# A two-layer decoder trunk on one core: a fourth lead unit with PSUM banks of its own, a new order of the lead's work, and the opening's square sums on POOL

## What is computed

```python
x = x + 0.5 * swiglu(rms_norm(x, n_ffn1), w_gate, w_up, w_down)      # 1024 -> 2816 -> 1024
x = x + concat(gmlp_chunks(rms_norm(x, n_mix)), rg_lru(...)) @ w_out
x = x + 0.5 * swiglu(rms_norm(x, n_ffn2), ...)                       # 1024 -> 2816 -> 1024
x = x + sigmoid(rms_norm(x, n_ple) @ w_ple_gate) * (p @ w_ple_proj)
# after the last layer: rms_norm(x, n_final)
# rms_norm(x, g) = x / sqrt(mean(x*x) + eps) * g;  swiglu = (silu(x@wg) * (x@wu)) @ wd
```

## Time and profile before

| | |
|---|---|
| median of 3 runs | 1858.75 us (1858.49 to 1860.04) |
| the profiled execution | 1858.88 us |
| its span, first to last instruction | 1857.2 us |
| granted PE clock, mean | 0.994 of full |
| busy: PE, DVE, ACT, POOL | 1819.7, 1508.2, 1063.0, 299.4 us |
| PE share of the chain of waits | 89% |
| DMA: weight loads by SP | 344 of 512 KB, median 3.8 us to landing |
| DMA: accumulating loads by POOL | 104 of 512 KB, median 6.4 us to landing |
| DMA: copy_lead by POOL | 4 of 520 KB, median 3.2 us to landing |

### The profile page before, as it was taken

One profiled execution on the slowest core, in us unless ns is written; L12 is line 12 of the kernel. 1 busy time (PEld: TensorE's weight loads), 2 busy tenths in 40 slices (PEclk: granted clock), 3 DMA queues, 4 the chain that ended last, 5 costly groups with the idle time before them and its releaser, 6 DMA issues.

```text
span 1857.2 us, 37525 instructions
## 1 busy us (share of the span) xinstructions
PE 1819.7 (98%) x14824; PEld 1797.5 (97%) x14824; DVE 1508.2 (81%) x2319; ACT 1063.0 (57%) x1538; POOL 299.4 (16%) x380
## 2 busy tenths in 40 slices
PE   7999999999999999999999999999999999999997
PEld 6999999998999999999999999999999999999997
DVE  7989978768689889787689789777775897988775
ACT  6656656545456566565466565554544665655553
POOL 0011011340120110112110110115202101011122
PEclk9999999999999999999999999999999999999998
DMA  5657579722346666795355765794223657667941
GB/s 173 155 151 188 136 199 246 216 80 69 110 134 155 175 166 152 194 262 172 124 148 127 197 167 158 209 249 147 71 92 114 162 137 194 158 160 230 237 140 47
DMA packets 81265, 297.16 MB, mean 160 GB/s; under 512 B 9344, under 2 KB 11680, under 8 KB 79312
## 3 DMA queue, kind: packets, MB, share of 16 engines
q1 hardware_dynamic: 52592, 184.87, 30.9%
q0 software_dynamic: 28512, 110.03, 27.8%
HBM read 267.00 MB, written 25.74 MB: 158 GB/s over the span
## 4 chain that ended last, share of the span: by engine, by line
PE 89%; DVE 7%; issue 2%; ACT 1%; DMA 0%; DVEq 0%; SPq 0%; ACTq 0%
PE main L764 24%; PE main L730 19%; PE main L769 12%; PE aux L764 9%; PE main L926 9%; PE aux L769 5%; PE aux L926 4%; PE aux L1028 2%; PE main L819 2%; PE aux L730 1%; PE aux L976 1%; DVE w_lo L1690 1%; PE main L1028 1%; PE aux L1048 0%; DVE tmp L1854 0%
## 5 line engine op out<-in xcount | busy, mean ns | idle before, releaser
L764 PE MATMUL main<-part_hi,w_hi 128*128 128x260 f32 x1296 | 328.5, 284 | 8.8 <-DVE tmp L1854 5.3
L764 PE MATMUL main<-part_lo,w_hi 128*128 128x260 f32 x1296 | 326.6, 283 | 0.0
L764 PEld LDWEIGHTS main<-part_hi,w_hi 128*128 128x128 f32 x1296 | 244.5, 189 | 11.6 <-DVE tmp L1854 7.7
L764 PEld LDWEIGHTS main<-part_lo,w_hi 128*128 128x128 f32 x1296 | 244.5, 189 | 0.0
L622 POOL DMA_DIRECT2D w_lo<-weights_dram x104 | 90.3, 868 | 851.1 <-ACT w_lo L1154 842.5
L769 PE MATMUL main<-part_hi,w_lo 128*128 128x260 f32 x1296 | 213.7, 282 | 0.2 <-DMA w_lo<-weights_dram 0.2
L1166 ACT ACTIVATE w_hi<-tau 128x1024 fp32r<-128x1024 f32 x104 | 109.9, 1057 | 177.0 <-PE main L769 152.4
L730 PE MATMUL main<-part_hi,w_hi 128*128 128x260 f32 x944 | 192.6, 285 | 2.0 <-DVE tmp L1738 2.0
L730 PE MATMUL main<-part_hi,w_lo 128*128 128x260 f32 x944 | 189.8, 283 | 0.0
L730 PE MATMUL main<-part_lo,w_hi 128*128 128x260 f32 x944 | 189.5, 282 | 0.0
L764 PE MATMUL main<-sig,w_hi 128*128 128x260 f32 x1280 | 181.6, 284 | 5.7 <-issue 5.7
(11 more groups left out here) (325 smaller groups left out, 4544.1 us busy)
## 6 DMA issues: line engine op xcount, KB each, us to landing
raw<-weights_dram SPq DMA_DIRECT2D x344, 512.0 KB, 3.8
w_lo<-weights_dram POOLq DMA_DIRECT2D x104, 512.0 KB, 6.4
d_part<-tmp POOLq DMA_DIRECT2D x64, 260.0 KB, 5.3
x<-d_part POOLq DMA_DIRECT2D x16, 1040.0 KB, 14.3
x_spill<-x POOLq DMA_DIRECT2D x6, 1040.0 KB, 4.9
x<-x_spill POOLq DMA_DIRECT2D x6, 1040.0 KB, 9.8
x<-x_in_dram SPq DMA_DIRECT2D x4, 520.0 KB, 6.7
x<-tmp POOLq DMA_DIRECT2D x4, 520.0 KB, 3.2
```

The costliest lines, as they stand in the source:

```text
L764: pe.matmul(ps, hi_w[:, w], xx(k), start=(start and k == 0 and b == 0), stop=False, skip_group_check=True)
```

## The change

Seven things change; the arithmetic does not.

1. The fourth lead unit gets a PSUM pair of its own, `aux[1]` (the list `FOURTHS`). PE then waits for it until the square root has read `aux[1]` (`std_s`) and no longer for gate_out(0). The `main` pairs shift by one: P1(0) waits for gate_out(0), P1(1) for hidden_out(0), and no longer for hidden_out(1).
2. copy_lead becomes two DMAs of one hidden tile each, with a semaphore each.
3. On ACT copy_p1(0) goes right behind hi12(0), and h_lead(1) from in front of copy_p1(0) to behind copy_p5(0).
4. On DVE tau3, tau4, hidden_out(1) and hidden_lo(0) leave the lead of all four stages: behind lo12(0) come tau3, tau4, hidden_out(1), lo34, hidden_lo(0), lo_b; hidden_lo(1) comes behind lo12(1).
5. The sums of pair 0 (raw and high part) are made after tile 0 instead of tile 2; the low parts of pairs 0 and 1 both after tile 2.
6. In the opening POOL adds the squares 3 to 7, DVE only 1 and 2; hi(3,3) and x21(0,0) go between ACT's squares.
7. In the opening the high parts of the first pair's sums come before the square root on ACT, and their low parts before the reciprocal on DVE.

```diff
+FOURTHS = tuple(t + 1 for t in THIRDS)
...
-SUM_ORDER = ((1, 0, 2, 3), (0, 1, 2, 3))
...
-    return (g + layer + (k >= G_GT + V_AFTER) + sum(g > t for t in THIRDS)) % 2
+    return (g + layer + (k >= G_GT + V_AFTER) + sum(g > t for t in THIRDS + FOURTHS)) % 2
...
-            return aux[0] if g in THIRDS else main[main_slot(g)]
+            return aux[0] if g in THIRDS else aux[1] if g in FOURTHS else main[main_slot(g)]
...
+            def copy_lead(f, G, k):
+
+                pool.wait_ge(evac, G - 2 * (LEAD - 1 - k))
...
-                pool.dma_start(x[:, XT - 2:XT, :], tmp[:, 2:4, :]).then_inc(lead_copy, 16)
+                pool.dma_start(x[:, XT - LEAD + k, :], T(2 + k)).then_inc(lead_copy[k], 16)
...
+            for o in range(3, XT):
+                add_square(pool, 0, o)
...
                     weights_in(n + 3)
-                    pe.wait_ge(evac, G + 1)
+                    pe.wait_ge(std_s, stat + 1)
                     acc(bank(G + 3), 3, XT, x_hi, x_lo).then_inc(unit, 1)
...
                         if first and t < 2:
-                            pe.wait_ge(evac, G - 2 * (1 - t))
+                            pe.wait_ge(evac, G - 3 + t)
...
-                        if t == 1:
+                        if c and t == 1:
                             pe.wait_ge(evac, G)
...
                         if stat == 0:
-                            x21(stat, 0)
+                            sigma_hi(stat, 0)
                             root(stat)
-                            sigma_hi(stat, 0)
...
                         hi12(n, S)
+                        copy_p1(0)
                         hi34(n, S)
                         act.wait_ge(sx_lo, 2 * KH * (2 * l + which + 1))
                         hi_b(n, S)
-                        h_lead(l, G - 2 * LEAD, 1)
...
                     copy_u2(0)
                     copy_p5(0)
+                    if first:
+                        h_lead(l, G - 2 * LEAD, 1)
...
             for o in range(2, XT):
                 prep(0, o)
-            hi(3, 3)
+                if o == 4:
+                    hi(3, 3)
+                if o == 5:
+                    x21(0, 0)
...
                         elif which:
...
                             gate_out(1)
                             sigma_lo(stat, 3)
-                            ahead(1, S0, S)
-                            ahead(2, S0, S)
-                            hidden_lo(0)
-                            hidden_out(1)
+                            tau1(S0, S)
+                            tau2(S0, S)
                         else:
...
                             tau1(S0, S)
                             tau2(S0, S)
-                            hidden_out(1)
                             sigma_lo(stat, 3)
-                            tau3(S0, S)
-                            tau4(S0, S)
-                            hidden_lo(0)
...
-                        if first and t == 2:
+                        if first and t == 0:
                             sums_raw(f, c, 0)
                             sums_raw2(f, c, 0)
...
-                        if not last and t >= pairs and k % 2:
+                        if not last and t >= pairs and k % 2 and not (first and t == 1):
                             sums_lo(l, f, c, k // 2)
                         if first and t == 2:
                             sums_lo(l, f, c, 0)
+                            sums_lo(l, f, c, 1)
...
                     if first:
                         lo12(n, S)
+                        tau_sums(0, (tau3, tau4))
+                        hidden_out(1)
                         lo34(n, S)
...
+                        hidden_lo(0)
                         lo_b(n, S)
...
             add_square(dve, 0, 1)
+            add_square(dve, 0, 2)
             lo(2, 2)
-            for o in range(2, XT):
-                add_square(dve, 0, o)
             lo(3, 3)
```

More of the change, by code:

```diff
@@ L309, in trunk @@
         sh_lo = sem("sh_lo")
-        lead_copy = sem("lead_copy")
+        lead_copy = [sem(f"lead_copy{k}") for k in range(LEAD)]
         d_second = sem("d_second")
@@ L667, in gates @@
                         if c == 0 and t == 1:
-                            copy_lead(f, G)
+                            for k in range(LEAD):
+                                copy_lead(f, G, k)
                         if c and t == 1:
@@ L1603, in sums_raw @@
                 if early:
-                    dve.wait_ge(lead_copy, 16 * (f + 1))
+                    for k in range(LEAD):
+                        dve.wait_ge(lead_copy[k], 16 * (f + 1))
                 if f:
@@ L1713, in free @@
                 pending[b] = False
-            def ahead(j, n, T_):
-                if j == 1:
-                    tau1(n, T_)
-                    tau2(n, T_)
-                    tau3(n, T_)
-                if j == 2:
-                    tau4(n, T_)
-                if j == 3:
-                    lo34(n, T_)
             def ffn(l, which, u0, g0):
@@ L1926, in ffn @@
                     lo12(n + 2, S + 1)
+                    if first:
+                        hidden_lo(1)
                     c11_r(0)
```

22 lines of the change are left out of this document (9 added, 13 removed).

## The result

| | before | after |
|---|---|---|
| median | 1859.09 us (1858.49 to 1860.04, 4 runs) | 1872.26 us (1871.67 to 1873.73, 4 runs) |
| the profiled execution | 1858.88 us | 1873.73 us |
| its span | 1857.2 us | 1872.0 us |
| granted PE clock, mean | 0.994 | 0.990 |
| busy: PE, DVE, ACT, POOL | 1819.7, 1508.2, 1063.0, 299.4 us | 1825.3, 1509.2, 1062.7, 310.1 us |

The changed kernel is slower: ratio 1.0072 with a 95% interval of 1.0057 to 1.0087. The forecast of 1868.0 had the sign and the place, but the median lies 0.26 us beyond the high end of the range. The profiled execution is the slowest of the four runs shown; its span is 14.8 us longer than before's, and the medians differ by 13.2. I account for the 14.8 here and come back to the spread, since it has a cause of its own.

The account below looks back on a forecast made before the run. PE, busy nearly the whole span, was taken to bound the kernel. Terms 2.7 + 2.7 + 0.15 - 0.65 + 6.0 - 1.7 = +9.2 us on 1858.88 gave 1868; low end 1860.5, high end 1872.

Parts of the forecast that it names:

- The path: P7(0) waits for copy_u2(0), behind gate(2) on ACT, whose weight load is issued after tau4: 6.13 us from tau4's end.
- B: Layer 0's second FFN stage: P7(0) at 559.96 instead of 557.30 us, +2.7 us.
- D: Layer 1's second FFN stage: P7(0) at 1472.09 instead of 1469.43 us, +2.7 us.
- A: The opening's FFN stage: P7(0) at 52.9 instead of 53.53 us, -0.65 us.
- C: Layer 1's first FFN stage: P7(0) at 966.35 instead of 966.20 us, +0.15 us.
- the clock stays up: Rival: same PE waits, but no clock fall in B, D and A, C as now; +2.8 us, 1861.7; chance 0.16.
- Faster: Rival: copy_u2(0) does not hold P7(0), so A and C keep what the banks give; 1848 us; chance 0.12.
- POOL is late: Rival: adds of 1.87 us make PE wait 1.6 in the third lead unit, shifting A's chain; 1869.5; chance 0.08.
- clock: PE at half clock behind gaps before P7(0): 1.6 us each in A, B and D, 1.2 in C; +6.0 us.
- sums: Early sums of hidden parts shorten PE's wait on c22(4): -0.4 us in each of four stages, -1.7 in all.
- part 3, the squares: Opening's five adds moved to POOL end at 25.2 us, costing some 0.2 before the root, covered by PE's third lead unit.
- the load: Weight load for tile 2's gate cut takes 3.5 us from SP's issue to landing; bound 0.3 later per stage.

Follow-up runs that it names:

- run 1: Changed kernel with tau3 and tau4 of tile 0 back in the lead, ahead of lo12(0), in all four stages: 1857.59 us, ratio to before 0.9989.
- run 2: Kernel before with only tau3 and tau4 of tile 0 moved behind lo12(0), in all four stages: 1868.42 us, one run.
- run 3: Changed kernel with copy_u2(0) and copy_p5(0) ahead of gate(2) on ACT in the first chunk: 1857.18 us, ratio to before 0.9989.
- run 5: Changed kernel, squares still on POOL; DVE waits for them before the first pair's sums, root and reciprocal ahead of that pair's halves and low parts: 1871.86 us.
- run 4: Changed kernel with squares 3 to 7 of the opening back on DVE, in front of lo(3,3): 1870.19 us, one run.
- run 6: Changed kernel with the second copy_lead transfer later, behind POOL's load for tile 2: 1872.97 us, one run.
- run 7: Changed kernel with the sums of pair 0 back after tile 2 and the low part of pair 1 back behind tile 1: 1873.05 us.
- run 9: As run 8, but the fourth lead unit in the main pair again, with PE's waits of the kernel before: 1863.17 us, one run.
- run 8: Changed kernel with the edits of run 1, run 3 and run 4 together: 1853.93 us, ratio to before 0.9971.
- run 10: As run 8, but with tau3 and tau4 left behind lo12: 1855.88 us, ratio to before 0.9985.

## Why the prediction was right and wrong

**Right.** The path: P7(0) on copy_u2(0) behind gate(2), on a load that waits for tau4. Runs 1, 2 and 3 show it link by link. The gap at P7 in B and D with no gap before, the vanished waits on gate_out and hidden_out, P6(0) early in A and C and its gain given back at P7(0), and a lost clock behind each gap all came as described. The rival "the clock stays up" fell: the clock fell in all four stages. "Faster" did not come, for the reason given against it; run 3 shows that it was one order of ACT's program away. "POOL is late", given a chance of 0.08, came nearly whole, beside the forecast and not in its place: PE waited 1.5 us where it had 1.6, and A came 1.8 later than forecast, though with two adds of 2.16 and 2.11 us and three of 1.3 instead of five of 1.87.

Term by term, in the profiled executions (14.8 us of span against the 9.2 of the sum):

| step | predicted | measured | how it is read |
|---|---|---|---|
| A, P7(0) | -0.65 | +1.12 | 54.65 against 53.53 |
| B, P7(0) | +2.7 | +3.2 | 10.40 behind P1(0) against 7.24 |
| C, P7(0) | +0.15 | +0.45 | 12.25 against 11.11, less 0.69 by which P1(0) no longer waits for gate_out in the lead |
| D, P7(0) | +2.7 | +2.8 | 10.05 against 7.24 |
| clock | +6.0 | +8.2 | P7(0) to P1(2): A 8.62 to 10.10, B 8.67 to 10.26, C 8.98 to 11.30, D 8.67 to 11.47 |
| sums | -1.7 | -0.8 | P1(2) to P4(4): 36.08, 36.07, 36.06, 36.07 to 35.88, 35.89, 35.88, 35.85 |

The measured column adds up to 15.0, 0.2 more than the span shows; where the 0.2 goes is open.

**The step that failed: A, and in it part 3, the squares.** I had POOL's chain end at 25.2, at a cost of some 0.2, and called the third lead unit its cover. It ended at 26.26, and PE waited for it (the first row of PE's timeline above); PE's sum over partitions then ran to 27.52, and the root cannot start before that. I also had the pace of DVE unchanged, "the sum of the fourth pair 0.5 earlier (41.86)". It ended at 43.55. The first pair's sums on DVE took 5.7 us instead of 1.8. On ACT this put the first pair's halves at 26.58 and the root behind them:

```profile
26.58 0.85 ACT L1151 ACTIVATE sig<-tmp 128x780 fp32r<-128x780 f32 x1 [2.53 <-DVE tmp L1659]
27.34 0.41 ACT L1152 ACTIVATE sig<-tmp 128x260 fp32r<-128x260 f32 x1
27.65 0.68 ACT L1209 ACTIVATE rstd_b<-aux,small 128x520 f32<-128x520 f32 x1
```

In the kernel before, the root began at 26.04. So the late adds alone would have held the root until 27.5, and DVE's stretched sums held it until 27.65. Run 5 agrees: there the sums take 0.49 but wait for the adds, the root starts at 27.18, and P7(0) still at 54.70. From there the stage runs as forecast, only later: tau4 ends at 48.52 where I had 46.75, and P7(0) follows 6.13 us behind it, exactly the distance in the prediction. So the whole 1.77 us error of A lies ahead of tau4, and run 4, which takes the adds off POOL, gives 1.60 back at tau4 (0.25 of it from before the squares) and 1.30 at P7(0).

The evidence was in the trace of before. There POOL also adds squares beside DVE's sums, in its timeline in layer 0, behind the mixing stage (POOL's row first):

```profile
517.05 1.59 POOL L509 TENSOR_TENSOR sum_home<-sum_home,rs 128x520 f32<-128x520 f32 x1 [4.09 <-ACT rs L1134]
...
517.40 1.53 DVE L1642 SCALAR_TENSOR_TENSOR tmp<-x,vecs,mix 128x260 f32<-128x260 f32 x1
518.86 0.48 DVE L1644 SCALAR_TENSOR_TENSOR tmp<-x,vecs,mix 128x260 f32<-128x260 f32 x1
```

The same instruction form takes 1.53 beside an add and 0.48 behind it. I had read POOL's min, median and max of the earlier trace rows as a property of POOL's add alone, and had not asked why one instruction of one shape takes 1.30 or 1.87. The high end of the range, 1872, was to take in the later load and late adds, and both came; with the smaller gain of the sums they make 1868 + 1.8 + 1.0 + 0.9 = 1871.7, which leaves no room for the clock below.

The Trainium skill has a sentence on it (SBUF — State Buffer, section "SBUF: two separate sides"): VectorE and GpSimd share one pair of SBUF interfaces, which is an exclusive lock, so that a VectorE instruction with two SBUF inputs and a GpSimd instruction that reads SBUF wait for each other whole. The rows of this case agree, as the last section shows in numbers; the forecast had left this rule out.

**B, C and D: the load, 1.0 us in all.** I took 3.5 us from the earlier trace rows, the only load at the right place; it was 4.0, 3.8 and 3.7. The prediction had named the bound (0.3 later per stage, if it meets its neighbours) and run 6 shows some 0.3 in C and D; what slows B is open. The rest of the chain, 2.42 on DVE, held within 0.01.

**The clock, 2.2 us.** I charged a fixed 1.6 per gap, read at one gap of before. A and B came to 1.5 and 1.6; C and D to 2.3 and 2.8 in this execution, with 6.83 us at 1.2 GHz. Run 7, with gaps of the same length, had 3.41 us in both, and so had runs 4, 5 and 6. Against the 8.67 us at full clock, the stages with 3.41 us at half clock lost 1.3 to 1.6 us and those with 6.83 lost 2.6 to 2.8, and which of them comes can differ from one execution to the next (the 2.3 of C is less the 0.3 that C lost here before the change). Less these 2.2 us the profiled execution would stand at 1871.5, beside the other three at 1871.67 to 1872.72. The sum priced the cheaper case rightly, the one in B, C and D of four of the five traces with these stops; the range lacked the dear one.

**The sums, 0.9 us.** I had 0.4 a stage. The wait at c22(4) fell by 0.3 and a stop of 0.1 opened earlier, which leaves 0.2, as run 7 shows. That the gap on c22 shrinks is as forecast; its size was half.

## What to carry to other kernels

Before a pair of instructions is moved behind a wait, follow what they release: two sums of 0.68 us cost 14.7 us here, because a load was issued on their last semaphore and an unrelated copy stood behind that load's first reader. Where an in-order engine has a short copy that the bound engine needs and a long instruction that waits for a DMA, the copy goes first; that one reordering turned the changed kernel from 0.7% slower to 0.1% faster. And where a row shows one instruction of one shape with two durations, look at what the neighbour engine does in each before either is used as a price.

## What the runs showed of the hardware

**VectorE and GpSimd take turns.** An add on POOL and a DVE instruction with both inputs in SBUF wait each other out, though their rows in the trace overlap. In the opening of the changed kernel POOL's adds start at 17.51, 19.81, 22.07, 23.52 and 24.98 and end at 19.67, 21.92, 23.38, 24.83 and 26.26. DVE's instructions end at 18.50, 20.76, 22.21, 23.66, 25.12 and 26.55. Each DVE end but the first two lies 0.28 or 0.29 us behind the end of an add, and each add ends 1.14 to 1.17 behind the end of a DVE instruction. The add that starts at 17.51, during a low part of 1.22 us that ends at 18.50, takes 2.16; the low part that starts at 19.01, while that add runs, takes 1.75 and ends 1.09 behind it. The same holds at 517 us before the change: the low part ends at 517.49, the add at 518.64 (1.15 later), the sum behind it at 518.94 (0.30 later). Alone, in run 5, an add takes 1.30 and a sum 0.49. So an add costs DVE about 1.04 us of its 1.31 (1.53 less 0.49), if DVE has such work at that time. DVE instructions with one input in PSUM show none of it: in the kernel before, 26 of them (tmp<-main,rstd_b and tmp<-aux,rstd_b, 128x520) run beside an add and take 0.68 to 0.70, as elsewhere. Moving adds of 0.70 us off DVE then saves it nothing: it was spared 3.5 us (five times 0.70) and lost 4.4, namely 5.81 less 1.95 on the four sums and 1.75 less 1.22 on the low part. POOL's median of 1.59 is not the add alone (1.30): the one at 517.05 starts 0.44 ahead of the low part's end and then takes its 1.15.

The Trainium skill (GPSIMD Engine Reference, section "Elementwise — side-by-side cycle accounting") gives 2.6 cycles per element, 1.13 us for this add as an estimate. Its rate is nearer to the chip than the prediction allowed: 1.14 to 1.17 behind a DVE instruction, 1.30 alone. What the rate leaves out is the waiting.

**A clock that falls for different times behind the same stop.** The stops are given here as PE's delay beyond its own pace, some 0.15 more than the profile's idle time. Behind a stop in B, C or D the granted clock went to 1.2 GHz, the lower of its two levels, for 3.41 us in some executions and for 6.83 in others: D's stop of 2.8 us cost 6.83 in the changed kernel and 3.41 in runs 4, 5 and 7. Nor does the length of the stop alone say whether it falls. A stop of 2.9 us in C left it at 2.4 GHz in run 1 and took it down in run 9; 2.6 us in D of run 6 and 2.7 in C of the kernel before took it down. In run 2 a stop of 1.95 us in front of P6(0) took it down in B, and one of 1.96 at the same product in D, with a second of 0.5 behind it, did not. The stops of up to 1.6 us behind the opening in runs 3, 8 and 10 did not. All stops of 3.1 us or more in B and C (changed kernel, runs 4 to 7) did.
